# Taking 39 products without a reader out of a two-layer decoder kernel

## The reference, cut to what matters

```python
# layer 0: dilated-window attention + cross-attention to a memory, output projection, then the dense SwiGLU
x = x + jnp.concatenate([mix, cross], axis=-1) @ w_out[i]
h = rmsnorm(x, ffn_norm[i])
x = x + swiglu(h, even_w_gate[j], even_w_up[j], even_w_down[j])        # 1024 -> 2816 -> 1024
# layer 1: an indexer scores all keys, each query keeps its top 64 of 256, attention over a low-rank latent of 256
h = rmsnorm(x, mixer_norm[i])
q, c_kv, q_idx, k_idx, w_idx, qc = split_cols(h @ odd_w_in[j], [...])
c_kv = rmsnorm(c_kv, odd_kv_norm[j])
mix = mixer_dsa(q, c_kv, q_idx, k_idx, w_idx, odd_w_uk[j], odd_w_uv[j], rel_bias)
...
h = rmsnorm(x, ffn_norm[i])
x = x + moe_swiglu(h, odd_w_router[j], ...)                            # top 2 of 8 experts, 1024 -> 3584 -> 1024
return rmsnorm(x, final_norm)
```

## Time and profile before

| what | value |
|---|---|
| runs | 1561.9, 1554.76, 1555.86 us |
| span of the profiled execution | 1555.8 us |
| PE busy | 1525.7 us, 98% |
| DVE busy | 1326.4 us, 85% |
| ACT busy | 1131.3 us, 73% |

### The profile page before, as it was taken

How to read it: one execution, slowest core, us unless ns; L and a number is a source line. 1 busy time by engine, 2 the same in 40 slices (tenths; PEclk the granted TensorE clock), 3 DMA queues, 4 the chain that set the end, 5 groups by cost and what they waited for, 6 DMA issues and landing times.

```text
span 1555.8 us, 25342 instructions
## 1 busy us (share of the span) xinstructions
PE 1525.7 (98%) x8159; PEld 1287.2 (83%) x8159; DVE 1326.4 (85%) x1806; ACT 1131.3 (73%) x1507; POOL 90.4 (6%) x68
## 2 busy tenths in 40 slices
PE   9999999999999999999999999999999999999997
PEld 8999967888887778888888888888888888888886
DVE  6888858777758778998998998998998998998997
ACT  6565556445547668788788788878888878878875
POOL 2422100000010000000000000000000000000000
PEclk9999999999999999999999999999999999999999
DMA  9944536666513477999999999999999999999993
GB/s 290 227 135 137 162 103 194 186 181 194 155 49 82 156 282 283 409 392 370 380 396 362 378 398 359 389 394 354 392 391 353 395 390 353 398 387 350 401 385 116
DMA packets 227061, 455.38 MB, mean 293 GB/s; under 512 B 12912, under 2 KB 120576, under 8 KB 227008
## 3 DMA queue, kind: packets, MB, share of 16 engines
q1 hardware_dynamic: 222800, 439.52, 78.4%
q0 software_dynamic: 4208, 15.22, 3.8%
HBM read 445.52 MB, written 9.18 MB: 292 GB/s over the span
## 4 chain that ended last, share of the span: by engine, by line
PE 91%; DVE 4%; ACT 3%; issue 1%; DMA 0%; SPq 0%; ACTq 0%; DVEq 0%
PE ps L740 26%; PE ps L742 26%; PE ps L741 26%; PE ps L991 5%; PE ps L993 2%; PE ps L1153 2%; PE ps L830 1%; PE ps L860 1%; ACT w_hi L1191 1%; DVE w_lo L1543 1%; DVE small L1632 1%; PE ps L845 1%; DVE z L1610 1%; DVE z L1629 1%; PE ps L1095 0%
## 5 line engine op out<-in xcount | busy, mean ns | idle before, releaser
L1543 DVE TENSOR_TENSOR w_lo<-big,w_hi 128x1024 fp32r<-128x1024 f32 x837 | 983.6, 1213 | 135.5 <-ACT w_hi L1191 59.6
L1456 ACT CAST w_hi<-big 128x1024 fp32r<-128x1024 f32 x672 | 693.6, 1056 | 139.5 <-PE ps L742 136.5
L740 PE MATMUL ps<-w_hi,m_hi 128*128 128x512 f32 (+1 forms) x1008 | 391.9, 389 | 1.4 <-ACT qT L1248 1.3
L741 PE MATMUL ps<-w_lo,m_hi 128*128 128x512 f32 (+1 forms) x1008 | 389.2, 386 | 0.0
L742 PE MATMUL ps<-w_hi,m_lo 128*128 128x512 f32 (+1 forms) x1008 | 389.2, 386 | 0.0
L740 PEld LDWEIGHTS ps<-w_hi,m_hi 128*128 128x128 f32 x1008 | 189.5, 188 | 41.4 <-issue 2.2
L742 PEld LDWEIGHTS ps<-w_hi,m_lo 128*128 128x128 f32 x1008 | 189.5, 188 | 38.4
L741 PEld LDWEIGHTS ps<-w_lo,m_hi 128*128 128x128 f32 x1008 | 189.6, 188 | 37.2
L1191 ACT CAST w_hi<-big 128x1024 fp32r<-128x1024 f32 (+1 forms) x171 | 166.0, 982 | 42.1 <-PE ps L742 36.7
L740 PE MATMUL ps<-w_hi,h_two 128*128 128x512 f32 (+1 forms) x464 | 182.6, 394 | 0.0
L742 PE MATMUL ps<-w_hi,h_two 128*128 128x512 f32 (+1 forms) x464 | 179.8, 387 | 0.0
(11 more groups left out here) (270 smaller groups left out, 1580.9 us busy)
## 6 DMA issues: line engine op xcount, KB each, us to landing
big<-in_odd_w_gate SPq DMA_DIRECT2D x112, 1024.0 KB, 7.3
big<-in_odd_w_up SPq DMA_DIRECT2D x112, 1024.0 KB, 7.4
big<-in_odd_w_down SPq DMA_DIRECT2D x112, 1024.0 KB, 7.4
big<-in_even_w_in SPq DMA_DIRECT2D x42, 512.0 KB, 4.6
big<-in_even_w_gate SPq DMA_DIRECT2D x22, 512.0 KB, 4.5
big<-in_even_w_up SPq DMA_DIRECT2D x22, 512.0 KB, 3.9
big<-in_even_w_down SPq DMA_DIRECT2D x22, 512.0 KB, 4.6
big<-in_w_out SPq DMA_DIRECT2D x20, 512.0 KB, 3.6
```

The lines of the kernel that those rows point to most:

```text
L740: mm(dst, a[0], b[0], start=start, stop=False, **kw)
L741: mm(dst, a[0], b[1], start=False, stop=False, **kw)
L1456: nc.scalar.copy(w_hi[:, slot, :], ring[s][:, (u % 2) * UNIT:(u % 2 + 1) * UNIT]).then_inc(s_hi, 1)
L1543: return V.tensor_tensor(dst, src, lead.bitcast(F32), ALU.subtract)
```

## The change

The helper and its five calls are removed: 12 + 8 + 8 + 8 + 3 = 39 products. Nothing else is touched; all waits, their order and all other instructions stay.

```diff
-            def keep_warm(n, bank):
-
-                two = h_two[:, 0, :, :].rearrange("p s n -> p (s n)")
-                for _ in range(n):
-                    mm(ps[:, bank, :], h_hi[:, 0, 0:P], two, start=True, stop=True)
-
...
-            keep_warm(12, 4)
             norm_turn(NORM_MIX1)
...
             def turn_latent():
 
-                keep_warm(8, 4)
                 pe.wait_ge(s_cch, 4)
                 for c in range(RC):
                     for t in range(TT):
                         last = tr(ps[:, 2, c * SEQ + t * P:c * SEQ + (t + 1) * P], cN[:, t, c * P:(c + 1) * P], ident)
                 last.then_inc(s_ctr, 1)
-                keep_warm(8, 4)
...
             next(turning).then_inc(s_lg, 1)
 
-            keep_warm(8, 2)
             pe.wait_ge(s_sl, 1)
...
             def gather_first():
 
-                keep_warm(3, 2)
                 pe.wait_ge(s_S, 1)
                 pe.wait_ge(s_xrow, TT)
```

## The result

| kernel | runs | median us | lowest to highest |
|---|---|---|---|
| before | 7 | 1557.44 | 1554.76 to 1561.9 |
| changed | 7 | 1561.15 | 1560.51 to 1564.61 |

The ratio is 1.0024, with a 95% interval of 1.0014 to 1.0035: the kernel without its 39 empty products is slower by 3.7 us, 0.24% (medians). That is within the 0.5% that the prediction called no change, and the interval excludes zero. The profiled execution has a span of 1558.7 us, 2.9 more than before. It took 1560.51 us: 1.8 us lie outside its span, as in every run of this study (1.75 to 1.85).

The account below looks back on a forecast made before the run. The prediction took the kernel to run at TensorE's pace, 98% busy, with the untouched experts 61% of the time. Terms 0.7 + 0.6 + 0.4 + 0 = +1.7 us on 1555.8 gave 1557.5 us, range 1554.0 to 1561.5.

Parts of the forecast that it names:

- The forecast's mechanism: At each of three emptied places between 425 and 593 us the clock falls about once to 1.2 GHz; chance 0.66.
- Place A: 12 products after the dense layer: nothing saved, a level fall costs 0.7 us, bounds 0 to 1.4.
- Place B: 8 products ahead of and 8 behind the latent's transposes: -0.8 us without a level fall, +0.6 with one; +0.6 taken.
- direct gain of 0.8 us: At the latent: transposes come earlier without the first 8 products, so VectorE starts c_lo 0.81 us earlier.
- Place C: 8 products behind the router's logits, 3 ahead of the first gather: +0.4 us, bounds -0.1 and +0.9.
- the rank products' delay: After the router: if the level falls before five rank products, VectorE's list and the experts start 0.8 us later.
- The existing low stretch: Low clock already at the index scores, 453.9 to 460.6 us: may shift, taken as 0, 1.4 us either way.
- The sum: All places from the dense layer to the experts: 0.7 + 0.6 + 0.4 + 0 = +1.7 us.
- nothing around the span: Whole execution: the profiled span of 1555.8 us was taken as the base time to which the sum is added.
- all on the path: Rival: all 39 products were on the path, so removing them saves 9.0 us, giving 1546.8 us; chance 0.03.
- the level holds: Rival: the empty products were never needed for the clock; only gains of 0.8 and 0.1 remain, 1554.9 us; chance 0.24.
- The long low level: Rival: at each of the three places the lower level lasts 6.7 us, giving 1564.5 us; chance 0.07.

Follow-up runs that it names:

- thin: All 39 empty products kept with their weight loads, but each streams 32 columns instead of 512, against the kernel before; ratio 1.0020.
- only_a: Only the 12 empty products behind the dense layer left out, against the kernel before; ratio 1.0010.
- before_again: The kernel before, run and profiled again with no edit; ratio 0.9995 against the kernel before.
- only_c: Only the 8 empty products behind the router and the 3 ahead of the gather left out, against the kernel before; ratio 1.0002.
- only_b: Only the 8 + 8 empty products around the latent's transposes left out, against the kernel before; ratio 1.0009.
- only_b1: Only the 8 empty products ahead of the latent's transposes left out, the 8 behind them kept, against the kernel before; ratio 0.9998.
- fitted: Against the kernel before, empty products only where PE waits, plus one ahead of each index head from the third on; ratio 1.0005.
- fitted2: Empty products only where PE waits, as in `fitted` but without the product per index head; ratio 1.0001 against the kernel before.

## Why the prediction was right, and where it was not

*The forecast's mechanism* (the level falls about once at each place) is shown: the low stretches stand behind the emptied gaps in both profiles of the changed kernel and in `thin`, and not at A or B in any profile of a kernel that kept the products there. It is also in the runs without a profile view. Over the 89 runs of the kernel before that stood beside the experiments the mean granted clock is 0.9961 and the mean time 1557.3 us; over the 18 of the changed kernel (both labels) they are 0.9904 and 1560.7. Within the kernel before alone, the 14 runs at 0.998 take 1555.1 us on average and the 13 at 0.994 take 1559.7.

*Place A*: 0.7 us forecast, 0.85 and 0.88 measured, in only_a 2.1 with a longer low stretch, above the bound of 1.4. The bound assumed that a fall lasts 3.3 us. The sum fits the mechanism, with other parts: the transposes themselves ran at half pace (1.94 us), so the first product came 1.90 us behind their start and not 1.65, and of the low stretch (to 434.60) only 1.2 us lay behind it, 0.5 us at 43%.

*Place B*: this step failed in one half. The level fell as forecast. The direct gain of 0.8 us was read from one profile, where the releaser of c_lo was ACT; in before_again and in only_c nobody keeps c_lo waiting. It was a consequence of the low stretch at the index scores, which the kernel before has in some executions only. With the upper level there, the 16 products are not on the path. A fall there alone costs 2.0 us (only_b, a low stretch of 6.7 us); the 1.1 us of only_b1 are mostly its empty products at the lower level. In the changed kernel the first softmax comes 24.1 us after the first index score, against 24.6 and 22.9 in the two profiles of the kernel before: 0.3 us more than their mean, where 0.6 was forecast.

*Place C*: 0.4 forecast, 0.86 and 0.88 measured against the first profile, 0.15 and 0.17 against before_again, where most of the gather ran at 0.50 too (C is 10.31). The number is near, but by luck: both readings of the step failed. It priced the rank products' delay, and that cost nothing, since VectorE's wait for ACT took it up (1.33 us before, 0.34 after) and the table of passes came 7.95 to 7.98 us after `sel` in all thirteen profiles. And it held the gather to be covered and m_lo to be what the first expert product waits for. With the level low for 10 us the gather ends at 10.3 us after `sel`, later than the list lets PE go on, and the index product and the first expert product follow it on PE. m_lo did wait 0.52 us, but the half of it that the first expert product waits for was finished at 595.36, 0.7 us ahead of that product. The low level itself came as forecast. Alone (only_c) the cost was nil, because there the gather started 0.6 us earlier after `sel` and the level was back 7.8 us after it.

*The existing low stretch*: taken as 0 with 1.4 either way; measured 12.5 us for I without it, 14.0 with 3.3 us of it, 15.0 with 6.7. Part of that is hidden behind VectorE: it starts on the best keys 9.03 us after the first index score without a low stretch and with 3.3 us of it, and 9.70 with 6.7. I + L of the kernel before is 22.9 or 24.6.

*The sum*: +1.7 us forecast; from the transposes to the first expert product the two profiles a side give 164.60 - 162.87 = +1.7 us, made of 0.9 at A, 0.3 at B with the index scores, and 0.5 at C. That it meets the forecast is partly chance: A and C came out higher, B lower. The runs' means say +3.4 (the two runs of the changed kernel, each against its own neighbours, +4.3 and +2.7). The other 1.7 us are not a place that the profiles leave out: the four profiled executions differ as wholes by only 1.6 us. The two of the kernel before took some 1557.6 and 1559.21 us, 1.1 above the mean of its runs, and the two of the changed kernel 1560.51 and 1559.43, 0.7 below. Two profiles a side cannot average over the courses; where the average execution of the changed kernel loses the rest stays open.

*The level of the forecast*: the step "nothing around the span" was wrong by 1.8 us. The profile's span of 1555.8 belongs to an execution of some 1557.6; that the median of three runs agreed with it was chance, for the median of seven is 1557.44. The measured 1561.15 lies 3.65 us above the forecast's 1557.5: 1.6 of it is the base, 2.0 the sum. It is inside the range, but 0.35 us from its upper end, and one of the seven runs (1564.61) is above it.

*The rivals*: all on the path (1546.8) is refuted by the ratio, the level holds (1554.9) by the stretches at 0.50. The long low level came true at place C, 10 us, and in only_a, but not at all three places at once.

## What to carry to other kernels

Before taking out work that nobody reads, look in the table of stretches at what the gap would hold without it and which level the clock has behind such gaps; here 39 empty products of some 9 us, nearly all beside other engines' work, were worth about 3.4 us. A wait seen in one profile may be the result of a low stretch that other executions don't have: profile the kernel before twice, and compare distances between events instead of spans. A delay on a path with a wait in it costs only what the wait does not take up: follow the list to the wait before pricing it. Filling a gap pays only where the engine is not itself a link of the chain that runs through it: between the index heads both an empty and a real product cost more than they saved.

## What the runs showed of the hardware

- The same kernel's executions differ in where the granted clock is low, and that is most of their scatter: 1554.26 to 1561.06 us over the 89 runs, with mean clocks from 0.999 to 0.994 (the correlation between a run's time and its mean clock is 0.90 in size).
- Weight loads and short products did not hold the level: the 39 with 32 columns each (median 263 ns by the profile, row below) left the same low stretches as none at all.

```profile
L763 PE MATMUL ps<-h_two x39: 178/263/396, 428.0 to 590.3; 128*128 128x32 f32 x39
```

- A product of 512 columns between two heads cost 0.38 us (`fitted` against `fitted2`) where its pace in a row is 0.23 us.
- Empty products that start after the level has fallen run at half pace and hold back what stands behind them: 8 took 3.28 us in only_b1, where the earlier trace rows have 2.09.
